# Feed-forward blocks of a two-part transformer kernel: seven of eleven hidden steps computed with the hidden columns on partitions

## The reference

```
D_FF = 2816

def swiglu(h, w_in, w_out):
    gate, up = jnp.split(h @ w_in, 2, axis=-1)
    return (jax.nn.silu(gate) * up) @ w_out

def second_block(x, norm_g, ...):
    for i in range(DEPTH_2):            # 4
        g = norm_g[i]
        x = x + 0.5 * rms_norm(swiglu(rms_norm(x, g[0]), ff1_w_in[i], ff1_w_out[i]), g[1])
        ...                             # the mixer of the layer
        x = x + 0.5 * rms_norm(swiglu(rms_norm(x, g[4]), ff2_w_in[i], ff2_w_out[i]), g[5])
```

## Time and profile before

| | |
|---|---|
| median of three executions | 2860.33 us (2856.72 to 2866.41) |
| the profiled execution | 2859.13 us, span 2857.3 us |
| mean granted TensorE clock | 0.982 |
| TensorE matmul busy | 2749.0 us, 96% |
| VectorE busy | 1597.7 us, 56% |
| ScalarE busy | 1233.5 us, 43% |

### The profile page before, as it was taken

The page is one execution under the profiler, slowest core; times in us unless marked ns, Lnnn a source line. Parts: engine busy times, 40 slices in busy tenths (PEclk is TensorE's granted clock), DMA queues, the critical chain, the costliest instruction groups (busy, mean ns, idle before and its releaser), DMA issues. The chain is left out here.

```text
span 2857.3 us, 35303 instructions
## 1 busy us (share of the span) xinstructions
PE 2749.0 (96%) x14506; PEld 2305.6 (81%) x14506; DVE 1597.7 (56%) x1821; ACT 1233.5 (43%) x1588; POOL 138.2 (5%) x227
## 2 busy tenths in 40 slices
PE   7988889999999999999998999999999999999998
PEld 6977877888788877888887888888878888896887
DVE  5884477776644535455554556455454554544544
ACT  3202256665534445344344435344453444445443
POOL 3000000000000100001000000000000010000000
PEclk9998989999999999999999999999999999999999
DMA  7532067887555435646544655554436555452652
GB/s 251 161 104 89 30 224 268 294 306 276 194 197 186 141 125 178 205 154 229 177 162 140 214 178 191 196 192 140 136 119 201 191 181 193 162 170 89 221 177 89
DMA packets 349485, 509.35 MB, mean 178 GB/s; under 512 B 14880, under 2 KB 295488, under 8 KB 349328
## 3 DMA queue, kind: packets, MB, share of 16 engines
q1 hardware_dynamic: 342960, 484.17, 50.4%
q0 software_dynamic: 5792, 20.78, 2.1%
q10 hardware_dynamic: 576, 2.20, 0.2%
HBM read 506.04 MB, written 1.05 MB: 177 GB/s over the span
## 5 line engine op out<-in xcount | busy, mean ns | idle before, releaser
L393 DVE TENSOR_TENSOR raw_r<-raw,whi 128x2048 fp32r<-128x2048 f32 x185 | 421.8, 2290 | 168.0 <-ACT whi L385 167.2
L833 ACT ACTIVATE h_hi<-psum 128x256 fp32r<-128x256 f32 x216 | 82.8, 383 | 758.1 <-PE psum L772 684.1
L385 ACT ACTIVATE whi<-raw 128x2048 fp32r<-128x2048 f32 x185 | 351.1, 1909 | 13.0 <-DMA raw<-in_w_up 7.4
L888 DVE TENSOR_TENSOR h_lo<-psum,h_hi 128x256 fp32r<-128x256 f32 x216 | 91.5, 423 | 439.0 <-ACT h_hi L833 439.0
L407 PE MATMUL psum<-place_lo,act_hi 128*128 128x512 f32 (+1 forms) x840 | 318.6, 379 | 0.0
L406 PE MATMUL psum<-whi,act_hi 128*128 128x512 f32 (+1 forms) x872 | 308.7, 354 | 5.4 <-DVE act_lo L639 4.3
L408 PE MATMUL psum<-whi,act_lo 128*128 128x512 f32 (+1 forms) x872 | 302.7, 347 | 0.0
L393 DVE TENSOR_TENSOR place_lo<-arena,place_hi 128x2048 fp32r<-128x2048 f32 x107 | 244.2, 2290 | 90.7 <-ACT place_hi L385 90.7
L407 PE MATMUL psum<-raw_r,act_hi 128*128 128x512 f32 (+1 forms) x808 | 284.2, 352 | 0.0
L406 PE MATMUL psum<-place_hi,act_hi 128*128 128x512 f32 (+1 forms) x592 | 234.1, 395 | 0.0
L408 PE MATMUL psum<-place_hi,act_lo 128*128 128x512 f32 (+1 forms) x592 | 228.6, 386 | 0.0
(11 more groups left out here) (537 smaller groups left out, 5820.6 us busy)
## 6 DMA issues: line engine op xcount, KB each, us to landing
arena<-in_ff_w_in SPq DMA_DIRECT2D x182, 512.0 KB, 5.0
raw<-in_ff_w_in SPq DMA_DIRECT2D x126, 512.0 KB, 4.8
arena<-in_ff_w_out SPq DMA_DIRECT2D x88, 512.0 KB, 4.5
raw<-in_ff_w_out SPq DMA_DIRECT2D x68, 512.0 KB, 4.4
wlo_f<-in_ff_w_in SPq DMA_DIRECT2D x44, 512.0 KB, 4.9
raw<-in_w_ada SPq DMA_DIRECT2D x20, 1024.0 KB, 5.2
raw<-in_w_gate SPq DMA_DIRECT2D x35, 512.0 KB, 4.4
raw<-in_w_up SPq DMA_DIRECT2D x35, 512.0 KB, 5.7
```

Of the source, the lines that this page charges most:

```text
L385: act.activation(hi, loaded, ACT.Copy).then_inc(S("slab_hi"), 1)
L393: dve.tensor_tensor(lo, loaded, hi.bitcast(F32), ALU.subtract).then_inc(S("slab_lo"), 1)
L833: act.activation(pair_of(turned_h[0], g), gate_up(g)[:, 0:256], ACT.Copy).then_inc(S("pass_turned_hi"), 1)
L888: dve.tensor_tensor(pair_of(turned_h[1], g), gate_up(g)[:, 0:256], pair_of(turned_h[0], g).bitcast(F32), ALU.subtract)\
```

## The change

Passes 4 to 17 of each block (`by_hidden`) are computed the other way round. A pass is now one step's 128 hidden columns (first or second half of the step's 256) for all 256 rows. In `ff_up` 128 weight columns are stationary, and the activations move: `act_hi` and `act_lo` are now the two halves of one buffer `act_both`, and one matmul moves 256 rows of both (512 columns) against the high part of the weights, a second moves 256 rows of `act_hi` against the low part. That is done for gate and for up, in a bank each: 32 matmuls, 16 of 512 and 16 of 256 columns. Each bank then holds two partial sums, side by side, of 256 columns each, with the hidden columns on partitions. VectorE adds them (`ff_sum_dve`) into `scratch` for gate and up at once, and silu, product, high copy and low part follow in SBUF. Nothing is turned. `ff_down` issues 12 matmuls as before: one 128-row piece of `w_out`, for both row tiles and both halves of the output. The passes take two banks each in place of one; the order of the splits beside them changes so that silu, product, copy and low part of pass n stand in its own turn, with one slab's split ahead of them and the second one (even passes) behind. The other eight passes of a block and everything outside the blocks keep their instructions.

```
+def by_hidden(n):
+    return 2 <= FF_PASSES[n][0] < FF_STEPS - 2
...
-        act_hi = sb("act_hi", [P, KD, T], F32R)
...
-        act_lo = sb("act_lo", [P, KD, T], F32R)
+        act_both = sb("act_both", [P, 2, KD, T], F32R)
+        act_hi, act_lo = act_both[:, 0, :, :], act_both[:, 1, :, :]
...
+        def sil_and_h(n):
+            return scratch[:, 3072:4096].rearrange("p (w n) -> p w n", w=2)[:, :, (n % 2) * 256:(n % 2 + 1) * 256]
...
+        def ff_banks_free(pe, f, n):
+            g = pass_no(f, n)
+            if by_hidden(n) and by_hidden(n - 2):
+                pe.wait_ge(S("pass_sum"), sums_before(f, n - 2) + 1)
...
         def ff_up(pe, f, n, half):
...
             for c in range(4):
                 k = 4 * half + c
-                ts = slice(t * P, (t + 1) * P)
-                last = three(pe, gate_up(g).rearrange("p (g n) -> p g n", g=2), (act_hi[:, k, ts], act_lo[:, k, ts]),
-                             (hi[:, c, :, :], lo[:, c, :, :]), k == 0, k == KD - 1)
+                if by_hidden(n):
+                    cs = slice(t * P, (t + 1) * P)
+                    for g in range(2):
+                        both = hidden_banks(n)[:, g, :, :]
+                        pe.matmul(both, hi[:, c, g, cs], act_both[:, :, k, :], start=k == 0, stop=False)
+                        last = pe.matmul(both[:, 0, :], lo[:, c, g, cs], act_hi[:, k, :], start=False, stop=k == KD - 1)
+                else:
...
         def ff_turn(pe, f, n):
+            if by_hidden(n):
+                return
...
+            for t in range(2) if by_hidden(n) else (part,):
+                for m in range(2):
+                    for j in (part,) if by_hidden(n) else range(2):
...
+        def ff_silu_act(act, f, n):
+            g = pass_no(f, n)
+            if by_hidden(n):
+                act.wait_ge(S("pass_sum"), sums_before(f, n) + 1)
...
             for n in range(2, LAST0):
-                if n > 2:
-                    turned_hi_act(act, pass_no(f, n - 1))
-                for j in FF_SPLIT[n]:
-                    slab_hi(act, name, j)
-                silu_act(act, pass_no(f, n))
+                if n in (3, 4):
+                    ff_hi_act(act, f, n - 1)
+                if by_hidden(n):
+                    slab_hi(act, name, FF_SPLIT[n][0])
+                    ff_silu_act(act, f, n)
+                    ff_hi_act(act, f, n)
+                    for j in FF_SPLIT[n][1:]:
+                        slab_hi(act, name, j)
...
+        def ff_sum_dve(dve, f, n):
...
+            dve.wait_ge(S("pass_gu"), g + 1)
+            dve.reduce_sum(sil_and_h(g), hidden_banks(n).rearrange("p g s t -> p g t s"), AX).then_inc(S("pass_sum"), 1)
...
+                if by_hidden(n):
+                    slab_lo(dve, name, FF_SPLIT[n][0])
+                    ff_sum_dve(dve, f, n)
+                    ff_h_dve(dve, f, n)
+                    ff_lo_dve(dve, f, n)
+                    for j in FF_SPLIT[n][1:]:
+                        slab_lo(dve, name, j)
...
+        def hidden_banks(n):
+
+            return psum[:, 4 + 2 * (n % 2):6 + 2 * (n % 2), :].rearrange("p g (s t) -> p g s t", s=2)
```

More of the change, by code:

```diff
@@ L164, in pass_no, with turned_before, sums_before @@
     return N_PASS + FF_N * f + n
+def by_hidden(n):
+    return 2 <= FF_PASSES[n][0] < FF_STEPS - 2
+N_TILED = sum(not by_hidden(n) for n in range(FF_N))
+def turned_before(f, n):
+    return N_PASS + N_TILED * f + sum(not by_hidden(q) for q in range(n))
+def sums_before(f, n):
+    return (FF_N - N_TILED) * f + sum(by_hidden(q) for q in range(n))
 FF_HEAD = (0, 1, 3, 4)
@@ L782, in ff_down @@
             hh, hl = (pair_of(ap, g) for ap in turned_h)
-            for m in range(2):
-                for j in range(2):
-                    js, ms = slice(j * P, (j + 1) * P), slice(m * 512, (m + 1) * 512)
-                    last = three(pe, acc[:, 2 * t + m, :], (hh[:, js], hl[:, js]), (hi[:, j, ms], lo[:, j, ms]),
-                                 i == 0 and j == 0, i == FF_STEPS - 1 and j == 1)
-                if m == 0 and i == FF_STEPS - 1:
-                    last.then_inc(S("y_ready"), 1)
+            for t in range(2) if by_hidden(n) else (part,):
+                for m in range(2):
+                    for j in (part,) if by_hidden(n) else range(2):
+                        at, ms = t if by_hidden(n) else j, slice(m * 512, (m + 1) * 512)
+                        js = slice(at * P, (at + 1) * P)
+                        last = three(pe, acc[:, 2 * t + m, :], (hh[:, js], hl[:, js]), (hi[:, j, ms], lo[:, j, ms]),
+                                     i == 0 and j == 0, i == FF_STEPS - 1 and j == 1)
+                    if m == 0 and i == FF_STEPS - 1:
+                        last.then_inc(S("y_ready"), 1)
             last.then_inc(S("pass_down"), 1)
@@ L844, in ff_act @@
             slab_hi(act, name, FF_SPLIT[1][0])
-            silu_act(act, pass_no(f, 0))
+            ff_silu_act(act, f, 0)
             if f:
```

149 lines of the change are left out of this document (96 added, 53 removed).

## The result

The changed kernel takes 2845.76 us (median of 4 runs, 2842.82 to 2846.02) beside 2860.47 for the kernel before (4 runs, 2856.72 to 2866.41). The ratio is 0.9939, with a 95% interval from 0.9925 to 0.9953. So it is 14.7 us faster, where 21.9 us were forecast. 2845.8 lies inside the range and between the forecast (2838) and the border of "no change" (2851.7), 2 us from the time of the rival "full stream price" (2844). The profiled execution took 2846.02 us. One execution of the kernel before, among those timed beside experiments 1, 2, 3 and 7, took 6939.63 us and is left out.

What follows compares the result with a forecast made beforehand. TensorE was taken as the bound. Transposes removed (-24.6 us) and dearer matmuls (+2.7) sum to -21.9: 2837.2 against the profiled execution, 2838 for the median; the 8-in-10 range was 2827 to 2852.

Steps and rivals of the forecast that it cites:

- no change: Rival: late vector work at pass 18 makes TensorE wait 2.8 us a block, 22 us, time 2860; chance 0.08.
- full stream price: Rival: a 256-column matmul costs 0.120 us beside a 512 too; gain 16.5 us, time 2844; chance 0.25.
- The bound: Mid-block, TensorE limits the kernel: at most 0.15 us of a pass's 8.54 could be waiting.
- The transposes: Removing them from 112 middle passes, 0.22 us each, gains 24.6 us.
- The matmuls: In `ff_up`, eight more matmuls for the same columns cost 0.024 us a pass, 2.7 us in all.
- s256: Price of a 256-column matmul in the new `ff_up`, taken as 0.117 us.
- s512: Price of a 512-column matmul in `ff_up`, taken as unchanged at 0.231 us.
- Cheap slabs: Rival: 4 ns of a 512-column matmul belong to the slab as moving operand; gain 29.1, time 2831; chance 0.07.
- The 4 ns: Gap between 0.231 us, the 512-column mean over slabs, and 0.227 over `raw` and `whi`; possibly 7.2 us more gain.
- Vector engines become the bound: Rival: a sum twice as long, 2.46 us, costs 49 us, time 2887; decides from 1.8 us; chance 0.08.
- the 15.55 against 16.7: Us for a step (two middle passes): vector engines' round against TensorE's need, leaving 1.1 us of air.
- the tightest place is the first middle pass: For the vector work: second half of step 3's `w_in` ready at 10.8, wanted at 13.9, 3 us later.

Runs made afterwards that it cites:

- experiment 1: The kernel before without the two transposes of each of the fourteen middle passes of a block: 2838.07 us, ratio 0.9922.
- experiment 2: The kernel after with the two 512-column matmuls of a piece first, then the two of 256: 2844.77 us.
- experiment 3: The kernel after with `act_both` laid out so a 512-column matmul moves one run of 512 instead of two of 256: 2849.94 us.
- Experiment 7: The kernel after with three 256-column matmuls for each slab piece, 48 in a pass instead of 32, same columns: 2855.16 us.
- experiment 4: The kernel after with VectorE's sum done twice in every middle pass: 2926.15 us.
- experiment 5: The kernel after with an extra VectorE sum of 0.68 us ahead of the sum in each middle pass: 2869.21 us.
- experiment 6: The kernel after with 0.68 us of extra sum in each middle pass, and the second split ahead of pass 18's silu and product moved behind them: 2854.85 us.
- 9: The kernel after with the two transposes of each middle pass put back, their result unused: 2877.20 us.
- 10: The kernel after, unchanged, timed once more: 2846.16 us, ratio 0.9957 to the kernel before.
- the first kernel of 8: The kernel after with `act_both` 8 KB lower in SBUF, in exchange with `act_f`: 2848.89 us.

## Why the prediction was right, and where it was off

**The bound: right.** TensorE was the limit before and is after, with no gap in the middle of a block.

**The transposes: right, 6% small.** 112 x 0.22 = 24.6 us were forecast, 26.2 measured by taking them alone away (0.234) and 24.8 by putting them into the other kernel (0.222). The 0.22 was read at one place and holds at all 112. The 1.5 us beyond it stand in the other matmuls of `ff_up`, 0.6 ns each, where the reading at the place can't see them.

**The matmuls: the step that failed in size.** The working took "s256 = 0.117, nearer to the seams but leaning to the stream, and s512 = 0.231 unchanged", with 0.024 us for a pass and 2.7 in all. The measured term is 8.4 us in the stretch and some 0.6 ahead of it, 9.0. From the means to the next start in the kernel after and in the kernel before without its transposes (the eight stretches hold 108 middle `ff_up` and 120 `ff_down`):

```
ff_up    16 x (232.8 + 117.1) - 24 x 230.4 = 5598 - 5530 = +69 ns, x 108 = 7.4 us
ff_down  12 x (231.3 - 230.7)                            =  +7 ns, x 120 = 0.9 us
sum                                                      8.3 us, of 8.4 measured
```

s256 was right to a tenth of a ns. s512 was not: the 512-column matmuls of the new `ff_up` cost 232.8, 2.4 more than those of the old one, and 16 x 2.4 = 38 of the 69 ns are theirs. A pair costs 350, as much as a 512-column matmul at 230.4 and a 256-column one at the 120 of the earlier trace rows would: what the first short matmul after a long one seemed to save in the earlier trace rows is not there in the sum. The working had this at hand as a bound only ("each of the 16 512-column matmuls dearer by 0.003"). Why the long ones cost more is not shown. The change of length alone doesn't do it (experiment 2: 232.7 ahead of a long one too), nor do the two runs (experiment 3). That activations move where weights moved before was not tried by itself. Experiment 7 prices the number of matmuls: 256-column ones alone cost 118.8, twice that is 237.6 for 512 columns.

**The rivals.** Full stream price: its size was right (8.1 us, 2844), its mechanism was not. A 256-column matmul beside a 512 costs 0.117 and not 0.120; the surcharge stands on the long ones. Cheap slabs: refuted. Over high slabs in `whi` and `wlo` the 512-column matmuls, now with the activations moving, went from 228.3 (experiment 1) to 234.9; over those in the arena they went from 233.7 to 229.8, and in the order of experiment 2 they have 232.3 and 233.4. The 4 ns belong neither to the slab as moving operand nor to the slab alone.

No change by the seam: not so. The product of pass 18 stood at 1742.10 in the fourth block, its turn at 1743.81, 1.7 us of margin where 2.2 were forecast (11.7 beside 13.9).

Vector engines become the bound: the sum took 1220 ns, so it did not come to pass, and the 15.55 against 16.7 of the working was right, as 1.16 us of waiting on VectorE shows. Experiments 4 and 5 show that the mechanism is there and the threshold about right: at 1.94 us for the sum the first cost appears. Its price was too low: "seven steps give 9.1, less 3 us of lead, so 6.1 us in each of 8 blocks" was for a sum of 2.46, and experiment 4, with such a sum, cost 9.8 in each. For the middle steps the working was right, in the rate (17.98 us for a step, 18.0 forecast) and in the lead: pass 18 starts 6.1 us late. What it left out is the seam behind them, the other 3.6 us: "the tightest place is the first middle pass" is wrong. The tightest is the seam at pass 18, with 1.7 us, and the working's own 2.2 there was already less than the 3 us of the first middle pass. Both gaps of experiment 5 stand at that seam, and experiment 6 took most of their cost away by moving one split.

The Trainium skill (PSUM — Partial Sum Buffer, section Specifications (TRN2)) says of PSUM's 8-byte lines that a non-contiguous pattern slows matmuls, and (SBUF — State Buffer, section Specifications (TRN2)) that each crossing to a new line pays a penalty. Neither speaks of a VectorE read of PSUM, to which the prediction stretched them; for such a read, a sum whose pairs stand 256 numbers apart, the trace shows no penalty: 1220 ns for 1024 numbers, where the contiguous read of 1024 took 1225.

The Trainium skill (TensorE: Matmul & The Clock Gate, section Back-to-back issue gap) would give, as an estimate by the formula that it calls the isolated gap, 109 + 216 = 325 ns for a pair. The runs show 350, and 230.4 for 512 columns alone, so the rows were the better base, for the price of the pair.

**The whole time.** -26.2 for the transposes and +9.0 for the matmuls are -17.2. The medians say -14.7. The missing 2.5 us lie outside the blocks: 2.6 us before the first block and 1.6 between the blocks in the two profiled executions. Neither touches changed code. Between the blocks three stretches, those before the second, the sixth and the eighth block, jump by 1.1 to 1.5 us from kernel to kernel (between the fifth and the sixth block 176.9 to 177.2 us for the kernel before and experiments 1, 4, 6 and 7, and 178.5 for the kernel after and experiments 2, 3, 5, 9, 10 and the first kernel of 8); whether the change is behind that, or an alignment of the DMA queues, was not tried. Of the 2.6 us I only know that the start of the first block moves between executions (784.46 and 785.29 for the same kernel, 781.9 to 789.9 over all kernels of the study) and in part along with the granted clock of the early stretch; the kernel before was profiled once, so whether it starts earlier as a rule is open.

What stays open is why a 512-column matmul between short ones costs 230 in one half pass and 235 to 237 in the next over the same slab (the rows at 1651.86 and 1660.28). It repeats exactly between executions and doesn't follow the runs of the moving operand or a shift of 8 KB. It does follow the order of the matmuls, in which places are dear though not in the mean: in the order of experiment 2 both of these half passes have 233.1. And it moves to other half passes when `act_both` stands behind the arena. None of the versions that compute the same beat the kernel after by more than 0.6 us in the blocks.

## What to carry to other kernels

When a change cuts the same columns into more matmuls, price each added matmul (here 6 to 9 ns), not the new shape alone, and don't take the price of a mixed stream from one seam between two lengths: here the pair of a long and a short one cost as much as each in its own stream. To price a removal, leave it out alone and measure between two marks that all kernels have; here that repeats to 0.01 us where whole times differ by 5. To price a wait, compare starts with starts: two brackets of 1.86 us stood for 2.26. And when an engine has air in the steady part, look for the place where its work piles up at the end of a block: three splits ahead of one product were the first to cost here, while the middle passes ran without a gap.

## What was new of the hardware

- A VectorE sum of pairs 256 numbers apart in PSUM takes as long as a contiguous read of the same size (1220 ns for 1024 numbers beside 1225 in the earlier trace rows), and 684 for 512 numbers.
- ScalarE takes 418 ns for 256 columns out of `scratch` and 384 for the same out of PSUM; on VectorE the product takes 425 out of `scratch` and 416 with one operand in PSUM.
- A pair of transposes costs 0.22 us at its place in a stream of 512-column matmuls; leaving 112 pairs out brought 0.234 each, putting 112 into the stream of mixed lengths cost 0.222 each.
- The distance of starts of 512-column matmuls differs from half pass to half pass (means from 227 to 237 ns in the fourth block) and repeats between executions.
- A bracket of 0.22 us of idle time between two matmuls cost 0.46 from start to start: the waiting matmul stood 0.61 behind its predecessor and the next one 0.30 behind it, in place of 0.23 each.
- The granted clock of the stretch with gaps (200 to 260 us) was 0.79 to 0.86 in the thirteen profiles. The five at 0.86 start the first block at 781.9 to 785.7 us, the eight at 0.79 to 0.83 at 787.2 to 789.9; within the second group the start does not follow the clock (787.2 at 0.79 in experiment 1, 789.1 at 0.83 in experiment 3).
